# Start addresses of the weight and stationary buffers, a later wait for the small loads, and two later transposes, in an encoder on one Trainium2 core

## The reference

```python
x = x + 0.5 * swiglu_ffn(rms_norm(x, ffn1_norm_g[l]), ffn1_w_gate[l], ffn1_w_up[l], ffn1_w_down[l])
h = rms_norm(x, mix_norm_g[l])
u = h @ w_in[l]
u_conv, c_q_raw, c_kv_raw, k_rope_raw, gl_conv, gl_mla = jnp.split(u, IN_SPLITS, axis=-1)
y_conv = conformer_conv_branch(u_conv, conv_w_dw[l], conv_b_dw[l], conv_ln_g[l], conv_ln_b[l], conv_w_pw_out[l])
y_mla = mla_branch(c_q_raw, c_kv_raw, k_rope_raw, cos, sin, mla_q_norm_g[l], mla_w_uq[l],
                   mla_kv_norm_g[l], mla_w_ukv[l], mla_w_o[l])
merged = jax.nn.sigmoid(gl_conv) * y_conv + jax.nn.sigmoid(gl_mla) * y_mla
x = x + merged @ w_out[l]
x = x + 0.5 * swiglu_ffn(rms_norm(x, ffn2_norm_g[l]), ffn2_w_gate[l], ffn2_w_up[l], ffn2_w_down[l])
```

## The kernel before

| tensor | before | rest by 64 | after | rest by 64 |
|---|---|---|---|---|
| `raw` | 1152 | 0 | 1184 | 32 |
| `w_hi` | 17536 | 0 | 17568 | 32 |
| `w_lo` | 33920 | 0 | 33952 | 32 |
| `h` | 66688 | 0 | 66752 | 0 |
| `hidden` | 112800 | 32 | 112896 | 0 |
| `attn`, `merged` | 131104 | 32 | 131200 | 0 |
| `c_kv` | 196640 | 32 | 196736 | 0 |
| `c_q` | 204832 | 32 | 204928 | 0 |

## Time and profile before

### The profile page before, as it was taken

One profiled execution on the slowest core, in us unless ns is written; L12 is line 12 of the kernel. 1 busy time (PEld: TensorE's weight loads), 2 busy tenths in 40 slices (PEclk: granted clock), 3 DMA queues, 4 the chain that ended last, 5 costly groups with the idle time before them and its releaser, 6 DMA issues.

```text
span 2373.1 us, 26781 instructions
## 1 busy us (share of the span) xinstructions
PE 2319.3 (98%) x10718; PEld 1926.1 (81%) x10718; DVE 1322.5 (56%) x1469; ACT 1188.6 (50%) x1619; POOL 0.2 (0%) x4
## 2 busy tenths in 40 slices
PE   5999999999999999989999999999999999999997
PEld 4888888888888888868889878888888888888886
DVE  4554544544544588978876455655544544544443
ACT  5444444444444577777767564445444444444433
POOL 0000000000000000000000000000000000000000
PEclk9999999999999999999999999999999999999999
DMA  6666666666655655546643456556656656656663
GB/s 229 192 189 187 192 189 188 193 187 185 186 184 182 194 188 186 181 147 203 192 146 116 132 164 184 186 179 203 194 186 189 192 187 189 193 186 186 187 188 131
DMA packets 120588, 432.65 MB, mean 182 GB/s; under 512 B 13584, under 2 KB 13840, under 8 KB 120208
## 3 DMA queue, kind: packets, MB, share of 16 engines
q1 hardware_dynamic: 120464, 430.93, 58.7%
HBM read 428.78 MB, written 2.10 MB: 182 GB/s over the span
## 4 chain that ended last, share of the span: by engine, by line
PE 96%; DVE 2%; issue 1%; ACT 1%; DMA 1%; SPq 0%; ACTq 0%; DVEq 0%
PE bank L663 31%; PE bank L662 31%; PE bank L661 31%; PE turned L672 2%; PE bank L799 1%; PE bank L773 1%; PE bank L774 1%; DMA pos_i<-in_pos_in 0%; DVE q_rope L1083 0%; DVE w_lo L900 0%; ACT w_hi L422 0%; DVE q_rope L1089 0%; PE turned L784 0%; DMA raw<-in_ffn_up 0%; PE turned L853 0%
## 5 line engine op out<-in xcount | busy, mean ns | idle before, releaser
L900 DVE TENSOR_TENSOR w_lo<-raw,w_hi 128x1024 fp32r<-128x1024 f32 (+2 forms) x814 | 987.1, 1215 | 995.0 <-ACT w_hi L422 994.6
L422 ACT ACTIVATE w_hi<-raw 128x1024 fp32r<-128x1024 f32 (+2 forms) x814 | 853.6, 1052 | 1039.1 <-PE bank L663 1035.8
L661 PE MATMUL bank<-w_hi,h 128*128 128x512 f32 (+1 forms) x2144 | 836.3, 390 | 28.0 <-DMA pos_i<-in_pos_in 26.4
L663 PE MATMUL bank<-w_hi,h 128*128 128x512 f32 (+1 forms) x2144 | 833.4, 389 | 0.0
L662 PE MATMUL bank<-w_lo,h 128*128 128x512 f32 (+1 forms) x2144 | 833.2, 389 | 0.0
L661 PEld LDWEIGHTS bank<-w_hi,h 128*128 128x128 f32 x2144 | 403.7, 188 | 110.8 <-DMA pos_i<-in_pos_in 26.4
L663 PEld LDWEIGHTS bank<-w_hi,h 128*128 128x128 f32 x2144 | 403.3, 188 | 82.7
L662 PEld LDWEIGHTS bank<-w_lo,h 128*128 128x128 f32 x2144 | 403.5, 188 | 81.6
L661 PE MATMUL bank<-w_hi,hidden 128*128 128x512 f32 x704 | 278.8, 396 | 0.0
L662 PE MATMUL bank<-w_lo,hidden 128*128 128x512 f32 x704 | 278.4, 395 | 0.0
L663 PE MATMUL bank<-w_hi,hidden 128*128 128x512 f32 x704 | 278.4, 395 | 0.0
(11 more groups left out here) (167 smaller groups left out, 1223.2 us busy)
## 6 DMA issues: line engine op xcount, KB each, us to landing
raw<-in_ffn_up SPq DMA_DIRECT2D x352, 512.0 KB, 4.0
raw<-in_ffn_down SPq DMA_DIRECT2D x176, 512.0 KB, 3.6
raw<-in_conv_in SPq DMA_DIRECT2D x64, 512.0 KB, 3.9
raw<-in_conv_gate SPq DMA_DIRECT2D x32, 512.0 KB, 4.0
raw<-in_mla_gate SPq DMA_DIRECT2D x32, 512.0 KB, 4.2
raw<-in_mla_out SPq DMA_DIRECT2D x32, 512.0 KB, 3.6
raw<-in_conv_out SPq DMA_DIRECT2D x32, 512.0 KB, 3.7
raw<-in_w_out SPq DMA_DIRECT2D x32, 512.0 KB, 3.6
```

Of the source, the lines that this page charges most:

```text
L422: act.activation(w_hi[:, j, 0:n], raw[:, j, 0:n], ACT.Copy).then_inc(hi_ready, 1)
L661: pe.matmul(dst, fixed_hi, moving_hi, start=first, stop=False)
L663: return pe.matmul(dst, fixed_lo, moving_hi, start=False, stop=last)
L900: dve.tensor_tensor(w_lo[:, j, 0:n], raw[:, j, 0:n], w_hi[:, j, 0:n], ALU.subtract).then_inc(lo_ready, 1)
```

## The change

It has five parts. (1) Three unused tensors of 32 bytes shift what is behind them: the three weight rings now begin 32 bytes past a multiple of 64, the stationary tensors at a multiple of 64. (2) TensorE's wait for the four small loads moves from its start to its first `turn_group` (group 1). (3) `x` is loaded in four pieces behind units 4 to 7 instead of in one behind unit 3; ScalarE's squares of `x` and the root follow one unit later; and a copy of two numbers goes ahead of ScalarE's first wait, with VectorE clearing its input. (4) Of the three query turns at `Q_END + 5` the third, and the key turn with it, move to `Q_END + 11`, on all three engines. (5) `BACK` is one unit later.

```diff
-TURNS = {"up": (2, 1, 1), "resid": (2, 2, 2), "glu": (2, 1, 0), "kv": (2, 2, 2), "q1": (3, 2, 2),
+TURNS = {"up": (2, 1, 1), "resid": (2, 2, 2), "glu": (2, 1, 0), "kv": (2, 2, 2), "q1": (2, 2, 2),
...
+LATE_TURN_AFTER = 11
...
+        self.q_turn = self.more_turns(1, 2, 2)
         self.k_turn = self.more_turns(1, 2, 0)
...
+        sb("before_weights", [P, 8])
         raw = sb("raw", [P, SLOTS, UNIT])
         w_hi = sb("w_hi", [P, SLOTS, UNIT], F32R)
         w_lo = sb("w_lo", [P, SLOTS, UNIT], F32R)
+        sb("after_weights", [P, 8])
...
+        sb("before_hidden", [P, 8])
...
-        FORE, BACK = M0 + 6, M0 + 20
+        FORE, BACK = M0 + 6, M0 + 21
...
                 load(u)
-                if u == 3:
-                    sp.dma_start(x[:, :, :], x_in).then_inc(x_loaded, 16)
+                if u >= 4:
+                    cols = slice(WIDE * (u - 4), WIDE * (u - 3))
+                    sp.dma_start(x[:, :, cols], x_in[:, :, cols]).then_inc(x_loaded, 16)
...
+            def take_late_turns():
+
+                act.wait_ge(turned, plan.q_turn + 1)
+                for r in range(2):
+                    act.activation(c_q[:, 4 + r, 0, :], turned_bank[plan.q_turn % 2][:, r * T:(r + 1) * T], ACT.Copy,
+                                   scale=gain["q"][:, 4 + r, :]).then_inc(turn_hi, 1)
+                t = turned_bank[plan.k_turn % 2]
+                act.wait_ge(turned, plan.k_turn + 1)
+                act.wait_ge(cleared, 4)
...
+            act.wait_ge(table_input, 1)
+            act.activation(root[:, :], total[:, :], ACT.Copy).then_inc(table_loaded, 1)
             act.wait_ge(gains_loaded, 16)
...
+                if u - AHEAD == Q_END + LATE_TURN_AFTER:
+                    take_late_turns()
-                if u == 8:
+                if u == 9:
                     take_root("x0")
-                if u in (6, 7):
-                    act.wait_ge(x_loaded, 16)
-                    tt = u - 6
+                if u in (7, 8):
+                    act.wait_ge(x_loaded, 64)
+                    tt = u - 7
...
+                if n == 1:
+                    pe.wait_ge(small_loaded, 64)
...
+            def late_turns():
+                pe.wait_ge(scaled, 4)
+                turn(plan.q_turn, cq_raw, 4 * P)
+                n = plan.k_turn
+                pe.wait_ge(*turn_freed(n - 2))
+                pe.wait_ge(key_step, 7)
...
-            pe.wait_ge(small_loaded, 64)
...
+                if u == Q_END + LATE_TURN_AFTER:
+                    late_turns()
...
+            dve.memset(total[:, :], 0.0).then_inc(table_input, 1)
...
+                if u - AHEAD == Q_END + LATE_TURN_AFTER:
+                    take_late_turns()
                 if u == 8:
                     variance("x0", 1, D)
+                if u == 9:
                     factor("x0", rstd)
```

More of the change, by code:

```diff
@@ L293, in encoder @@
         scaled = sem("scaled")
+        table_input = sem("table_input")
+        table_loaded = sem("table_loaded")
         xt_hi = sem("xt_hi")
@@ L493, in take_turns @@
                         act.activation(q_rope[:, k:k + 2, 0, :], pair, ACT.Copy).then_inc(turn_hi, 1)
[L494 to L500, removed]
+            def take_late_turns():
[6 more added lines that the diff above has]
+                act.wait_ge(cleared, 4)
+                for j in range(2):
+                    rows = slice(ROPE * j, ROPE * (j + 1))
+                    act.activation(k_rope[rows, j, :], t[rows, 0:T], ACT.Copy).then_inc(turn_hi, 1)
             def make_tap(n):
@@ L691, in turn_group @@
                     turn(g.turn + b, src, 2 * P * b + (WIDE * g.i if g.kind in ("resid", "merge") else 0))
[L692 to L699, removed]
+            def late_turns():
[4 more added lines that the diff above has]
+                pe.wait_ge(key_step, 7)
+                for tt in range(2):
+                    last = pe.transpose(turned_bank[n % 2][:, tt * P:(tt + 1) * P],
+                                        k_rot[:, tt, :, :].rearrange("p d c -> p (d c)"), identity[:, :])
+                last.then_inc(turned, 1)
             def low_turned(stage, kinds, k):
@@ L733, in wait_stationary @@
                 elif g.stage == "q_rope":
-                    t = turns[plan.stage("latents")[2].turn + 2]
+                    t = turns[plan.q_turn]
                     pe.wait_ge(turn_lo, t.lo_before + t.lo)
@@ L950, in finish @@
                     if g.stage == "ffn1_down" and g.i == 0:
-                        dve.wait_ge(x_loaded, 16)
+                        dve.wait_ge(x_loaded, 64)
                     for tt in range(2):
@@ L1040, in take_turns, with take_late_turns @@
                                                      op1=ALU.subtract).then_inc(turn_lo, 1)
+            def take_late_turns():
+                dve.wait_ge(turn_hi, turns[plan.q_turn].hi_before + 2)
+                for r in range(2):
+                    dve.scalar_tensor_tensor(out=c_q[:, 4 + r, 1, :], in0=turned_bank[plan.q_turn % 2][:, r * T:(r + 1) * T],
+                                             scalar=gain["q"][:, 4 + r, :], in1=c_q[:, 4 + r, 0, :], op0=ALU.mult,
+                                             op1=ALU.subtract).then_inc(turn_lo, 1)
             def clear_once():
```

## The result

| | before | changed |
|---|---|---|
| median | 2375.38 us (2374.39 to 2376.43, 5 runs) | 2386.33 us (2386.25 to 2387.66, 5 runs) |
| span of the profiled execution | 2373.1 us | 2384.5 us |
| TensorE busy | 2319.3 us | 2358.4 us |

The changed kernel is slower by half a percent: 1.0048 times the time of before, 95% interval 1.0036 to 1.0059. The forecast was 2317 us, 2.5% faster, with a range of 2260 to 2348.

The account below looks back on a forecast made before the run. TensorE's own work was taken to bound the kernel. Savings of 18.2, 10.6, 1.5, 19.2 and 9.3 us sum to 58.8, taking 2375.1 to 2316.3, or 2317 us on the median's scale; range 2260 to 2348.

Parts of the forecast that it names:

- The start: TensorE's first matmul no longer waits for the last small load and starts at 8.2 us instead of 26.45: -18.2 us.
- `BACK`: One unit later, it removes TensorE's 1.5 us idle in the turns of `conv_tok`: -1.5 us.
- The supply: Loads and splits of the first units keep up with TensorE; a rival had units 5 to 8 late, within 2300 to 2328.
- The tightest point: Unit 8 at the start, ready near 31 us and wanted at 31.7; costed at nothing, 3 us kept in the range.
- The late turns: Moved `cq_raw` turns end TensorE's 8.47 us idle and the half clock behind it: -10.6 us, bounds -8.5 and -11.1.
- Stationary operands at a multiple of 64: `hidden`, `attn`, `merged`, `c_q`: 2952 matmuls save 6.5 ns each by the new start: -19.2 us, bounds 0 and -19.2.
- Rings 32 bytes past one: Shifted weight rings as moving operand save 1 ns on each of 9288 matmuls of 512 columns: -9.3 us.
- The rings' new place costs: Rival: a moving operand straddling lines stalls, 6.6 ns more per matmul, giving 2388 us; chance 0.14.
- The excess mostly goes: Rival: shifting one operand frees much of the 13.4 ns excess per matmul; half gives 2264 us, all 2202; chance 0.18.
- Addresses do nothing: Rival: the longer steps have another reason, so only start, turns and `BACK` gain 30.3 us: 2346 us; chance 0.08.

Follow-up runs that it names:

- e2_old_places: The changed kernel with all three 32-byte shifts taken out, so every tensor lies where it lay before; 2345.36 us, ratio 0.9873.

## Why the prediction was wrong

**The start, -18.2, and `BACK`, -1.5: right.** 19.8 us together by the difference of two kernels, 17.9 and 1.7 by their traces. The supply held: TensorE's whole wait for `w_lo` at L684 is 9.9 us, 8.3 of them ahead of its first matmul, the rest among the taps. The tightest point was unit 8. Its split ends at 30.79 us, near the 31 forecast, and TensorE reaches it at 32.80, where 31.7 was forecast:

```profile
29.56 1.23 DVE L929 TENSOR_TENSOR w_lo<-raw,w_hi 128x1024 fp32r<-128x1024 f32 x1 [2.59 <-ACT w_hi L434]
```

**The late turns, -10.6: right**, 10.6 us by themselves, in an interval of 7 to 14.

**Stationary operands at a multiple of 64, -19.2: wrong.** The step that failed is the reading of the earlier trace rows: "what differs is that `h` begins at a multiple of 64 bytes and `hidden` 32 past one". Something else differed as well and was the cause: `h` lay a multiple of 256 bytes behind the rings, the other four 32 or 416. In a kernel whose rings begin at a multiple of 64 the two readings can't be told apart by 64, so the agreement of the five tensors said nothing for one reading over the other. In the change `hidden` went from distance 32 to 96 and lost 1.0 ns instead of winning 6.5; 2112 x 1.0 is +2 us.

**Rings 32 bytes past one, -9.3: wrong.** The step that failed is the price of 1 ns won, taken from the row "nearest" in its pair of alignments, the `heads` row of 256 columns. Its alignments were those of the change, but they are not what counts; the row lies at distance 96, while `h` came to 32, and at 256 columns the places rank differently than at 512. Moving the rings took `h` from distance 0 to 32: 6336 matmuls of 512 columns times 6.5 ns is +41 us where the forecast had -9. By the traces of the changed kernel and of `e2_old_places` the stages with stationary `h` are 39.6 us longer, those with `hidden` 2.0 longer, and those from `c_q` to `attn` 0.7 shorter: 41 us, as the two times say. In sum: 2375.8 - 10.6 - 19.8 + 41.0 = 2386.4 us.

**The rivals.** "The rings' new place costs" gave 2388 us and the measured time is 2386; its size, 6.6 ns, is that of the step that `h` gained. But its mechanism, a moving operand that straddles lines, as far as alignment to 64 goes, is refuted: with rings and stationary tensors both 32 past a multiple of 64 `h` steps at 226.8 ns. It hit the time by a coincidence of counts: it charged 9288 matmuls from a base in which `hidden`, `attn`, `merged` and `c_q` had become fast, while in truth they stayed slow and only the 6336 with `h` became slower. "The excess mostly goes" found no support: 226.7 ns is the least at any distance tried. "Addresses do nothing" is refuted by 41 us. The Trainium skill, "TensorE: Matmul & The Clock Gate", section "What happens when you issue a matmul", says that loading the next weights doesn't take bandwidth from the running matmul; that alone would make places a matter of nothing, and the runs here do not bear it out: the steps go from 226.7 to 234.3 ns with the distance between what is streamed and what is loaded.

**What stays open.** The runs show that the distance by 256 bytes sets the step, not what in the chip couples the two reads. That the load of the next stationary operand beside the running matmul is the partner is inferred from the distance's two ends; the rows of the loads do not show it, at 187.5 to 188.7 ns on average with `h`, `hidden`, `attn` and `merged` at every multiple of 32 tried. Work of VectorE and ScalarE beside it is not what costs: in the changed kernel, from 50 us on, the steps with `h` average 234.9 ns where VectorE and ScalarE both stand still (274 steps) and 233.4 where both are busy (919 steps), against 226.7 and 227.1 before. DMA writes were not told apart in this way. Why 13.4 ns above the 213.3 of 512 columns remain at the best place was not found.

## What to carry to other kernels

When TensorE bounds a kernel and its matmuls stream and load from SBUF at full rate, compare steps between stages with the same shapes; if they differ, tabulate the first bytes of both operands of each stage and look at their difference, not at each one's alignment. Here placing every stationary tensor a multiple of 256 bytes from the streamed rings took 18 us off 2345 at the cost of a few hundred unused bytes per partition, while shifting one side by 32 bytes cost 41 us. At 256 columns another distance was better, so each shape needs its own look. And before several rows that agree are counted as several pieces of evidence, ask what else they share: here all of them shared the ring.

## What the runs showed of the hardware that was not expected

- The step of a matmul of 512 fp32r columns with its 128x128 stationary operand depends on the distance between the two operands' starts, with a period of 256 bytes: 226.8 ns at 0, 228.9 at 192, 232.4 to 234.3 at the other multiples of 32.
- Absolute placing did not matter in the one case tried: shifting rings and stationary tensors together by 32 bytes left each step the same within 0.1 ns.
- At 320 columns the distance cost nothing: 146.6 ns with `h` at 0, 146.7 at 32. At 256 columns 0 is not the best place: 119.5 to 120.0 ns there, 116.4 to 117.9 with the latents at 448.
- At distances of 16 and 240 bytes the step has more than one value, 226.7 or 233.3 and 226.7 or 228.3, kept for whole uninterrupted stretches and changed only at interruptions; the time of the kernel with these places spreads by 17 us.
